# A mixture-of-experts stage: the experts' gate-and-up products in halves of 32 tokens, the second half under a branch

## What is computed

```
def _moe(h, w_router, b_router, w1, w3, w2):       # h: 256 x 1024
    scores = jax.nn.sigmoid((h @ w_router).astype(jnp.float32))
    ...                                             # two experts for each token
    for e in range(N_EXPERTS):                      # 16
        he = jax.nn.silu(h @ w1[e]) * (h @ w3[e])   # w1, w3: 1024 x 512
        out = out + gates[:, e:e + 1] * (he @ w2[e])  # w2: 512 x 1024
    return out
```

## Time and profile before

| | us |
|---|---|
| median of 3 runs (lowest to highest) | 988.1 (986.34 to 995.4) |
| the profiled execution's own time | 996.42 |
| its span (first to last instruction) | 994.6 |
| TensorE busy in it | 936.2 (94%), mean granted clock 0.986 |
| the 16 DMA engines: moved | 230.74 MB, mean 232 GB/s |

### The profile page before, as it was taken

The page is one execution under the profiler, slowest core; times in us unless marked ns, Lnnn a source line. Parts: engine busy times, 40 slices in busy tenths (PEclk is TensorE's granted clock), DMA queues, the critical chain, the costliest instruction groups (busy, mean ns, idle before and its releaser), DMA issues.

```text
span 994.6 us, 11764 instructions
## 1 busy us (share of the span) xinstructions
PE 936.2 (94%) x4268; PEld 513.5 (52%) x4269; DVE 416.4 (42%) x894; ACT 304.7 (31%) x693; POOL 31.4 (3%) x54
## 2 busy tenths in 40 slices
PE   3999999999998999987999999999989999999998
PEld 1464456565443344332455445455765546577763
DVE  1279597634461012421222322601956633336452
ACT  3200534232412213340322331312465632125420
POOL 0100200000000000000000002000000000000000
PEclk9999999999999999997999999999989999999999
DMA  9998614488559799898799999404227724423401
GB/s 350 362 386 316 141 58 173 161 318 320 204 222 337 239 360 387 299 392 318 278 396 393 397 378 307 154 31 159 87 86 252 224 74 169 169 88 111 130 13 42
DMA packets 105693, 230.74 MB, mean 232 GB/s; under 512 B 3125, under 2 KB 6505, under 8 KB 105497
## 3 DMA queue, kind: packets, MB, share of 16 engines
q1 hardware_dynamic: 100288, 217.85, 61.8%
q0 software_dynamic: 2208, 7.37, 2.6%
q10 hardware_dynamic: 3128, 4.62, 1.4%
HBM read 224.31 MB, written 5.51 MB: 231 GB/s over the span
## 4 chain that ended last, share of the span: by engine, by line
PE 78%; DVE 8%; DMA 6%; ACT 4%; issue 2%; SPq 1%; POOLq 1%; ACTq 0%; POOL 0%; DVEq 0%
PE bank L646 23%; PE bank L913 12%; PE bank L926 6%; PE bank L660 5%; DMA arena<-in_w_mod_dram 5%; PE bank L943 4%; PE bank L1221 3%; PE bank L1150 3%; PE bank L1240 2%; PE bank L1231 2%; PE bank L612 2%; DMA arena<-in_gla_w_in_dram 1%; PE bank L842 1%; PE bank L938 1%; PE bank L775 1%
## 5 line engine op out<-in xcount | busy, mean ns | idle before, releaser
L646 PE MATMUL bank<-arena 128*128 128x512 f32 (+3 forms) x592 | 238.0, 560 | 4.3 <-DMA arena<-in_gla_w_in_dram 2.3
L646 PEld LDWEIGHTS bank<-arena 128*128 128x128 f32 x592 | 111.8, 191 | 122.5 <-issue 110.4
L913 PE MATMUL bank<-arena 128*64 128x512 f32 x512 | 114.6, 600 | 2.9 <-issue 2.9
L660 PE MATMUL bank<-arena 128*128 128x256 f32 (+1 forms) x384 | 99.1, 416 | 2.8 <-ACT arena L1945 1.5
L660 PEld LDWEIGHTS bank<-arena 128*128 128x128 f32 x384 | 72.1, 190 | 30.6 <-issue 21.4
L913 PEld LDWEIGHTS bank<-arena 128*64 128x64 f32 x512 | 39.4, 139 | 74.5 <-issue 73.8
L926 PE MATMUL bank<-arena,con 128*64 128x512 f32 x272 | 67.7, 644 | 4.7 <-ACT con L1848 4.0
L2395 DVE TENSOR_TENSOR con<-con,bank 128x256 f32<-128x256 f32 x17 | 7.1, 420 | 111.1 <-ACT con L1753 111.1
L1749 ACT ACTIVATE con<-bank 128x256 f32<-128x256 f32 x17 | 6.5, 384 | 139.9 <-PE bank L913 139.9
L926 PEld LDWEIGHTS bank<-arena,con 128*64 128x64 f32 x272 | 22.3, 147 | 39.7 <-issue 38.6
L612 PE MATMUL bank<-arena,silu_c 128*32 128x512 f32 x272 | 35.9, 652 | 5.6 <-DMA arena<-in_w_mod_dram 4.1
(11 more groups left out here) (415 smaller groups left out, 1207.1 us busy)
## 6 DMA issues: line engine op xcount, KB each, us to landing
arena<-in_w_gate_e_dram SPq DMA_DIRECT2D x16, 2048.0 KB, 14.5
arena<-in_w_up_e_dram SPq DMA_DIRECT2D x16, 2048.0 KB, 13.2
arena<-in_w_down_e_dram SPq DMA_DIRECT2D x16, 2048.0 KB, 12.8
arena<-in_w_mod_dram SPq DMA_DIRECT2D x12, 2048.0 KB, 16.4
arena<-in_mod_w_dram SPq DMA_DIRECT2D x12, 2048.0 KB, 8.2
arena<-in_ab_w_in_dram SPq DMA_DIRECT2D x7, 2048.0 KB, 9.2
arena<-in_gla_w_in_dram SPq DMA_DIRECT2D x6, 2048.0 KB, 16.2
arena<-in_cd_w_in_dram SPq DMA_DIRECT2D x6, 2048.0 KB, 7.8
```

The lines of the kernel that those rows point to most:

```text
L646: mm = pe.matmul(ps[:, 0:n], lhs[:, k, tile * P:(tile + 1) * P], w[:, k, c0:c0 + n], start=(k == 0), stop=(k == kd_ - 1))
L660: mm = pe.matmul(ps[:, i * n:(i + 1) * n], w[:, k, c * P:(c + 1) * P], rhs[:, k, 0:n], start=(k == 0), stop=(k == KC - 1))
L913: mm = pe.matmul(up_b[64 * j:64 * j + 64, :], h[:, k, :], blocks[:, g + n:u + n + 1:u - g, :], start=(k == 0), stop=(k == KC - 1), tile_po ...
```

## The change

The first product of an expert becomes `up_half`: 32 of the 64 tokens, in 8 chunks times 4 column groups (32 columns of the array each, all four at the same time), 256 moving columns in each call, so 32 calls for a half. The bank `up_b` holds the two halves of the tokens in its columns 0 to 255 and 256 to 511, and in each of them 128 gate and 128 up columns; the sigmoid, the gated product and the copy of the transposed result get access patterns for this, without a further instruction. Half 1 (tokens 32 to 63) stands under a branch; half 0 is always computed, behind it. Expert 0 always computes both.

Which branches are taken follows from one number per expert, `passes`: 0 up to 32 tokens, 1 up to 64, 2 up to 128 and so on. VectorE computes it in five instructions. TensorE loads it once for each expert (in the place of the first flag) and uses it for half 1 and for the surplus blocks. The loop of three rounds over the surplus blocks now stands ahead of every expert's product (from expert 1 on), with no branch around it; its rounds load no flag, and an empty round raises one semaphore by 3 in the place of three drains. The three semaphores of the surplus (up, transposes, down) are merged into one, `x_step`.

```
@@ TensorE @@
+            def up_half(h, half, e, gathered=False):
+                g, u = (slot_at(s) // P for s in expert_slot[e][0:2])
+                for k in range(KC):
+                    if gathered:
+                        pe.wait_ge((hg_a, hg_v)[k % 2], k // 2 + 1)
+                    for j in range(4):
+                        n = 4 * k + j
+                        mm = pe.matmul(up_b[32 * j:32 * j + 32, 256 * half:256 * half + 256],
+                                       h[:, k, HALF * half:HALF * half + HALF], quarters[:, g + n:u + n + 1:u - g, :],
+                                       start=(k == 0), stop=(k == KC - 1), tile_position=(0, 32 * j))
+                return mm
...
-            def extras(e):
+            def extras(e, blocks_of_e):
                 with pe.Fori(0, EXTRA) as t:
-                    n = t + e * EXTRA
-                    flag = pe.value_load(flags[:, bass.ds(n, 1)], min_val=0, max_val=1)
-                    with pe.If(flag > 0):
+                    with pe.If(blocks_of_e > t + 1):
+                        n = t + e * EXTRA
                         pe.wait_ge(x_h, n + 1)
-                        up(hs_x, e, x_up)
+                        up(hs_x, e, x_step)
                         pe.wait_ge(x_ff, n + 1)
-                        turn_ff(x_turned)
+                        turn_ff(x_step)
                         landed_expert(e, 2)
                         pe.wait_ge(x_ffT, n + 1)
-                        down(e, x_down)
+                        down(e, x_step, False)
+                        pe.drain()
                     with pe.Else():
-                        pe.drain().then_inc(x_up, 1)
-                        pe.drain().then_inc(x_turned, 1)
-                        pe.drain().then_inc(x_down, 1)
+                        pe.sem_inc(x_step, 3)
...
                 if e == 0:
-                    up(hg[:, :, 0:CAP], e, up_done, True)
-                any_extra = pe.value_load(flags[:, e * EXTRA:e * EXTRA + 1], min_val=0, max_val=1)
+                    up_half(hg, 1, e, True)
+                    up_half(hg, 0, e).then_inc(up_done, 1)
+                blocks_of_e = pe.value_load(passes[0:1, e:e + 1], min_val=0, max_val=1 + EXTRA)
...
-                with pe.If(any_extra > 0):
-                    extras(e)
-                with pe.Else():
-                    no_extras()
+                extras(e, blocks_of_e)
                 pe.wait_ge(hs_ready, e)
-                up(hs[e % 2], e, up_done)
+                with pe.If(blocks_of_e > 0):
+                    up_half(hs[e % 2], 1, e)
+                up_half(hs[e % 2], 0, e).then_inc(up_done, 1)
                 behind_up(e)
                 ctx_work(CTX_WORK_BEHIND.get(e, []))
@@ ScalarE @@
-                sigmoid(sig_step, 2 * e).then_inc(silu_done, 1)
+                sigmoid(sig_step, 2 * e, up_b[:, :].rearrange("p (a g c) -> p g a c", a=2, g=2)[:, 0],
+                        act1.rearrange("p (a c) -> p a c", a=2)).then_inc(silu_done, 1)
@@ VectorE @@
+            link(dve.tensor_scalar(rank[:, 0, :], cnt, float(HALF), None, ALU.is_gt))
+            for t in range(EXTRA):
+                link(dve.scalar_tensor_tensor(rank[:, 0, :], cnt, float(CAP * (t + 1)), rank[:, 0, :], ALU.is_gt, ALU.add))
+            dve.tensor_copy(passes[:, :], rank[:, 0, :])
             for t in range(EXTRA):
                 dve.tensor_scalar(extra_flag[:, :, t], cnt, float(CAP * (t + 1)), None, ALU.is_gt)
```

More of the change, by code:

```diff
@@ L34 @@
 CAP = 64
+HALF = CAP // 2
 EXTRA = T // CAP - 1
@@ L218, in build @@
         extra_flag = sb("extra_flag", [P, NE, EXTRA], I32)
+        passes = small[:, 352:352 + NE].bitcast(I32)
         first_slot = small[:, 288:288 + NE * (1 + EXTRA)].rearrange("p (e t) -> p e t", t=1 + EXTRA).bitcast(I32)
@@ L225, in build @@
         blocks = arena[:, :].rearrange("p (n c) -> p n c", c=256)
+        quarters = arena[:, :].rearrange("p (n c) -> p n c", c=P)
         def view(off, *dims):
@@ L275, in build @@
         act1, act2, ffT = spent[:, 0:256], spent[:, 256:512], spent[:, 512:768].rearrange("p (c s) -> p c s", c=2)
+        ff_halves = spent[:, 512:768].rearrange("p (q a s) -> p a q s", q=4, a=2)
         y_buf = [gate_rows[:, 0, 0:512], gate_rows[:, 0, 512:1024]]
@@ L525, in build, with x_upped, x_turned, x_downed @@
         sink_exp = sem("sink_exp")
+        def x_upped(n):
+            return n * 3 + 4
+        def x_turned(n):
+            return n * 3 + 5
+        def x_downed(n):
+            return n * 3 + 6
         block = ctx.enter_context(nc.Block())
@@ L920, in turn_ff, with down @@
                 mm.then_inc(sem_, 1)
-            def down(e, sem_):
+            def down(e, sem_, whole):
                 w2 = view(slot_at(expert_slot[e][2]), 4, D)
                 for kc in range(4):
+                    c, at = (kc // 2, 64 * (kc % 2)) if whole else (kc % 2, 64 * (kc // 2))
                     for q in range(2):
-                        mm = pe.matmul(dn_b[64 * q:64 * q + 64, :], ffT[:, kc % 2, 64 * (kc // 2):64 * (kc // 2) + 64],
+                        mm = pe.matmul(dn_b[64 * q:64 * q + 64, :], ffT[:, c, at:at + 64],
                                        w2[:, kc, 512 * q:512 * q + 512], start=(kc == 0), stop=(kc == 3),
@@ L1092, in behind_up @@
                 pe.wait_ge(ffT_ready, e + 1)
-                down(e, down_done)
+                down(e, down_done, True)
             for e in range(NE):
@@ L1112, in _ @@
                         behind_up(e)
-                    pe.wait_ge(x_down, EXTRA)
+                    pe.wait_ge(x_step, x_downed(EXTRA - 1))
                     continue
-                with pe.If(any_extra > 0):
-                    extras(e)
-                with pe.Else():
-                    no_extras()
+                extras(e, blocks_of_e)
                 pe.wait_ge(hs_ready, e)
-                up(hs[e % 2], e, up_done)
+                with pe.If(blocks_of_e > 0):
+                    up_half(hs[e % 2], 1, e)
+                up_half(hs[e % 2], 0, e).then_inc(up_done, 1)
                 behind_up(e)
@@ L1401, in wait_free @@
                     if e0 == 0:
-                        sp.wait_ge(x_down if j0 == 2 else x_up, EXTRA + (0 if j0 == 2 else 1))
+                        sp.wait_ge(x_step, x_downed(EXTRA - 1) if j0 == 2 else x_upped(EXTRA - 1))
                 elif s == 0:
@@ L2551, in _ @@
                 dve.wait_ge(up_done, e + 1)
-                gated(silu_done, e + 1, up_gated, e).then_inc(ff_ready, 1)
+                both = up_b[:, :].rearrange("p (a g c) -> p g a c", a=2, g=2)
+                gated(silu_done, e + 1, up_gated, e, both[:, 0], both[:, 1], act1.rearrange("p (a c) -> p a c", a=2),
+                      act2.rearrange("p (a c) -> p a c", a=2)).then_inc(ff_ready, 1)
                 behind_ff(e)
@@ L2872, in _ @@
             stage_extra(0)
-            pool.wait_ge(x_up, 1 + EXTRA)
+            pool.wait_ge(x_step, x_upped(EXTRA - 1))
             with pool.Fori(0, NE // 2 - 1) as i:
```

45 lines of the change are left out of this document (21 added, 24 removed).

## The result

The changed kernel is slower: 998.8 us median of 11 runs (997.43 to 1002.09) against 989.68 us (986.34 to 995.4). The ratio is 1.0088, with a 95% interval of 1.0068 to 1.0107. I had forecast 980.0 us, with a range of 970 to 992, and put "slower" at 0.12.

The account below looks back on a forecast made before the run. TensorE and two trains of weight loads at the memory's pace were taken to bind. Expert 15's product 6.2 us earlier, -3.43 for its half and +1.7 for half clock gave -8.0 us: 980.0 from 988.1, range 970 to 992.

Parts of the forecast that it names:

- the branch around half 1 adds 0.2: Sequencer cost ahead of each expert's product: the new branch adds 0.2 us, part of 2.3 us more from landing to matmul.
- The trains: Two runs of expert weight loads at the memory's pace, each started when a product frees a slot, limit the gain.
- the first train: Weight loads from 330.0 us on: expert 5's product starts at 389.5 against 397.07, 7.6 us earlier.
- The second train: Weight loads behind expert 8's product, full to the end: expert 15's product starts at 578.4 against 584.64, 6.2 us earlier.
- My -8 us: Sum for the whole kernel: -9.7 us at expert 15 with +1.7 for half clock gives -8.0 us.
- The cost of a half: Each expert's first product: a half takes 3.43 us, 3.7 at most; nine skipped halves save TensorE 30.9 us.
- The packing figure: Skill's speedup of 3.07 for four row tiles: a half would take an estimated 4.5 us; the prediction did not adopt it.
- The empty rounds: Three surplus rounds ahead of each product: 0.9 us each; 0.1 to 0.4 exposed, 2.3 where weights are late, 1.8 at expert 7.
- Half clock at expert 15: Expert 15's half, after TensorE stood waiting for weights, runs at half clock: some +1.7 us.
- VectorE's five instructions: Ahead of the gather's evictions: they make expert 0's product about 1.0 to 1.2 us later, taken as +1.2.
- rival D: Slower: the surplus loop's way back fetches instructions anew, 28 us partly covered, 8 gained, about 1003 us; chance 0.12.
- The base: Profiled execution of before at 996.4 us becomes 988.4; the same -8 applied to the median 988.1 gives 980.0.

Follow-up runs that it names:

- half 0 first and the loop: The changed kernel with half 0 computed ahead of the branch around half 1, the surplus loop still ahead of every expert: 985.37 us, ratio 0.9906.
- half 0 first and one branch: The changed kernel with half 0 computed ahead of half 1's branch and the surplus loop behind one branch: 981.55 us, ratio 0.9929.
- the last experiment: Half 0 first, one branch around the surplus, and a quarter of the expert weights' bytes after each slot's first filling: 966.92 us, ratio 0.9738.
- the kernels with the stalls covered: The two kernels that compute half 0 ahead of half 1's branch, with the loop or one branch around the surplus: ratios 0.9906 and 0.9929.
- the second profile of before: Another profiled execution of the kernel before, with nothing changed: 991.17 us, expert stage ending at 593.6 us.
- both halves with the loop: The changed kernel with half 1 computed for every expert, no branch around it, the surplus loop still ahead of every expert: 999.4 us, ratio 1.0087.
- the loop alone: The changed kernel with the whole product of 16 calls restored, the surplus loop still ahead of every expert: 994.6 us, ratio 1.0045.

## Why the prediction was wrong, point by point

**The step that failed** is one line under the costs: "the branch around half 1 adds 0.2". I priced the branch as an instruction and half 1, where it is skipped, at nothing. It is 128 instructions that must be passed, right behind 112 others that are passed as well, and the code behind them must be fetched while the weights' loads fill the DMA engines. This cost 3.1 + 4.4 + 2.7 us at experts 2 to 4, 1.7 at expert 9, 0.6 at expert 12, 1.6 behind expert 13, 1.4 of the 2.4 at 14 and about 3.5 of the 5.9 at 15 (the rest there is rounds behind late weights), and half clock behind the stalls of experts 2, 3, 14 and 15. Nowhere did I ask how many instructions a us the new form uses: a half passes 128 instructions in 3.66 us, where `up` passed 64 in 6.9.

**The trains.** Half right, where the stall is out of the way. With half 0 first and the loop, expert 5's up matrix landed at 365.5 + 18.4 = 383.9 us and its product started at 387.6; I had 385.8 and 389.5.

```profile
L1394 SPq DMA_DIRECT2D arena<-in_w_up_e_dram x1: 3817/3817/3817, 365.5 to 365.5; - x1
...
DMA to landing us min/median/max: 18.4/18.4/18.4
...
385.10 2.50 issue
387.60 8.84 PE bank L934 x128
```

In the changed kernel it started at 397.55, because TensorE had lost the time itself before the loads could bind. Expert 8's product ended at 475.4 (forecast 471.4), expert 15's started at 590.7 (578.4). With half 0 first and one branch nothing waited at expert 5 (386.67, above), so the first train bound only together with the rounds. The second train bound as forecast, by the windows of the last experiment. My -8 us are what the kernels with the stalls covered gained (-0.7% to -0.9%). But with half 0 first and one branch expert 8's own product ended at 462.7 us, 9.6 earlier than in the second profile of before, where I had 6.4; so that the sums agree is in part luck.

**The cost of a half.** 3.66 us alone, 7.15 for both: at my upper bound, 3.7, rather than at 3.43, so nine halves skipped and seven pairs at 7.15 save some 27 us and not 30.9. The packing figure of the Trainium skill, "TensorE: Matmul & The Clock Gate", Part 3, by which it would be an estimated 4.5 us, is not borne out by this row (556.72, 3.66).

**The empty rounds.** 0.90 us each was right: the heads of the three rounds ahead of expert 2 run from 335.2 to 337.0 us, two rounds in 1.8. From landing to product it is 3.7 us (496.5 to 500.2 at expert 10), as forecast. What I took for exposed, 1.8 us at expert 7, was 1.7:

```profile
L980 PEldq COMPARE_BRANCH  x3: 218/221/221, 335.2 to 337.0; - x3
```

**Half clock at expert 15.** I gave it 1.7 us. The half took 6.61 us in the place of 3.66, so it was 2.95.

**VectorE's five instructions.** They took 0.91 us, from 286.43 to 287.34 on its timeline. Expert 0's product ended 9.9 us behind the selection matrix, against 8.7 in both profiles of before, so the 1.2 was right.

**The prediction's rival D** had the right kind of mechanism and the wrong place. It had the loop's way back fetch anew; the 45 executions of that branch took 0.24 us at most:

```profile
L979 PEldq COMPARE_BRANCH  x45: 86/224/239, 319.7 to 587.0; - x45
```

It is the way forward that costs. D was also dismissed for a reason that doesn't hold for this: "branches over such distances are there before, and the longest took 0.33 us". One jump over 112 instructions was free before, by those rows; two in a row were not measured by any row of before. The rule of the Trainium skill, "Runtime: NRT & Kernel Launch", section "Instruction fetch mechanics", that a taken branch whose target is outside the fetched window waits for a fetch, fits the rows of L1136. That sentence deserved a rival of its own for half 1.

**The base.** The profiled execution of before carried half clock that the second doesn't, and the stage of the second profile ends 5 us earlier. My sum went by differences, so this moved the forecast little; it would have misled who compares two single profiles (996.4 and 998.7).

**What stays open.** The runs don't show at which instruction a fetch is asked for, only when it starts and lands, so how long a fetch is held up by traffic is not known. At experts 1 and 13 the branch itself took 0.2 us, but neither was quite free: expert 1's half took 4.09 us and not 3.66, and behind expert 13's stand the 1.62 us. And the 5 us by which both halves with the loop exceed the loop alone are only partly seen.

## What to carry to other kernels

Work that is skipped still has to be passed: count the instructions between two products, and how long the engine's own work covers the passing. Where a stall has no cause among the waits, set it beside the times of the instruction fetches. Where a branch may skip much, put it behind work that is always done, not ahead of it, and not behind another long jump. And read for each saving which train of loads stands behind it: here TensorE was busy for 29 us less, and with whole loads no version that ran gained more than about 9.

## What the runs showed that I had not expected

- A conditional branch that takes 0.2 us took up to 5.7 us (with one branch around the surplus) when it followed another jump over some 110 instructions, and a stall inside a product moved by exactly the 64 instructions by which the code was moved.
- Each of the changed kernel's stalls ended 1.3 to 1.6 us behind the landing of a fetch of 16 KB. The same holds for the branches of the experiments: of the 24 executions over 0.6 us in the expert stages of all runs, each ended 1.3 to 1.5 us behind one.
- With a quarter of the loads' bytes they stayed where the DMA share ahead of the product was 0.91 or more (3.8 us at expert 3) and were gone where it was 0.51 or less (3.1 us became 0.3 at expert 2).
- Four column groups of 32 with 256 columns each gave 3.66 us for what a whole product of two groups does in 6.9 for twice the tokens, a loss of 6%.
- In the changed kernel waits of 3.79 and 2.38 us on TensorE were followed by a product that was in part at half clock (8.8 us instead of 7.1 at expert 10, 5.35 instead of 3.66 at expert 14), and waits of 2.67 and 2.63 us were not (experts 4 and 8). Two executions of the kernel before differed in this after the same wait (2.60 and 2.59 us, then 8.74 and 7.11 for the same product).
